# DeltaNet inverse on one core: the next D of a level by a product and a VectorE sum instead of a transpose

## The reference, cut to what matters

```python
def _gdn_chunked(q, k, v, beta, g, s0):
    ...
    decay = jnp.exp(jnp.where(incl, gc[..., :, None] - gc[..., None, :], -jnp.inf))
    kb = k * beta[..., None]
    lmat = jnp.where(strict, jnp.einsum("bhnik,bhnjk->bhnij", kb, k) * decay, 0.0)
    tinv = lax.linalg.triangular_solve(eye + lmat, jnp.broadcast_to(eye, lmat.shape), left_side=True,
                                       lower=True, unit_diagonal=True)
    u = tinv @ (v * beta[..., None])
    w = tinv @ (kb * jnp.exp(gc)[..., None])
    ...
```

## Time and profile before

| | |
|---|---|
| median of 3 runs | 2289.26 us (2286.62 to 2290.01) |
| profiled execution, its own time | 2281.79 us |
| its span, first to last instruction | 2279.9 us |
| PE busy | 2070.7 us (91%) |
| DVE busy | 984.4 us (43%) |
| ACT busy | 535.7 us (23%) |
| POOL busy | 267.5 us (12%) |
| mean granted clock of PE | 0.953 of full speed |
| inverses and chains of the 8 heads | 733 to 1412 us of the span |

### The profile page before, as it was taken

One profiled execution on the slowest core, in us unless ns is written; L12 is line 12 of the kernel. 1 busy time (PEld: TensorE's weight loads), 2 busy tenths in 40 slices (PEclk: granted clock), 3 DMA queues, 4 the chain that ended last, 5 costly groups with the idle time before them and its releaser, 6 DMA issues. The chain is left out here.

```text
span 2279.9 us, 28981 instructions
## 1 busy us (share of the span) xinstructions
PE 2070.7 (91%) x11714; PEld 1230.2 (54%) x11714; DVE 984.4 (43%) x1928; ACT 535.7 (23%) x1299; POOL 267.5 (12%) x333
## 2 busy tenths in 40 slices
PE   3799999999978999999999988999999794999985
PEld 1555555555544666667667665556555443443432
DVE  4355546556554465565654653000000186222224
ACT  1231423314212434344334343000000000111111
POOL 0020020110201111111021021000000000321102
PEclk9899999999989999999999999999999895999998
DMA  8120021201102101101011011982440734699973
GB/s 307 53 65 23 24 65 47 56 10 47 47 0 79 29 15 42 29 15 31 19 37 29 16 42 47 321 230 83 132 117 1 263 148 194 236 398 404 401 316 143
DMA packets 177812, 260.05 MB, mean 114 GB/s; under 512 B 14759, under 2 KB 146664, under 8 KB 163344
## 3 DMA queue, kind: packets, MB, share of 16 engines
q1 hardware_dynamic: 151096, 218.91, 28.0%
q10 hardware_dynamic: 18488, 23.54, 3.6%
q0 software_dynamic: 8096, 15.75, 1.9%
HBM read 231.65 MB, written 39.10 MB: 119 GB/s over the span
## 5 line engine op out<-in xcount | busy, mean ns | idle before, releaser
L678 PE MATMUL bank<-hT,shared 128*128 128x512 f32 x384 | 188.1, 619 | 7.8 <-DMA shared<-in_w_in_dram 7.8
L1504 PE MATMUL bank<-hT,shared 128*128 128x512 f32 x384 | 169.3, 594 | 2.6 <-DVE xT L1877 1.8
L2476 PE MATMUL bank<-ring,xgT 128*64 128x512 f32 (+1 forms) x416 | 150.2, 627 | 13.2 <-DMA ring<-in_w_exp_up_dram 10.1
L1559 PE MATMUL bank<-wz,hT 128*128 128x512 f32 x320 | 153.7, 618 | 0.0
L2058 DVE SCALAR_TENSOR_TENSOR prod<-gth,bank 128x512 f32<-128x512 f32 x16 | 11.0, 688 | 272.1 <-PE bank L2028 272.1
L1504 PEld LDWEIGHTS bank<-hT,shared 128*128 128x128 f32 x384 | 71.1, 190 | 84.5 <-issue 84.3
L2028 PE MATMUL bank<-yT,wm 128*128 128x512 f32 x256 | 111.2, 592 | 0.0
L2476 PEld LDWEIGHTS bank<-ring,xgT 128*64 128x64 f32 (+1 forms) x416 | 57.0, 165 | 95.6 <-issue 95.6
L1270 DVE TENSOR_TENSOR X<-bank,negm 128x512 f32<-128x512 f32 (+1 forms) x120 | 67.8, 598 | 91.3 <-PE bank L754 91.0
L678 PEld LDWEIGHTS bank<-hT,shared 128*128 128x128 f32 x384 | 67.3, 192 | 67.4 <-issue 54.7
L2028 PE MATMUL bank<-hT,wm 128*128 128x512 f32 x224 | 98.0, 595 | 0.0
(11 more groups left out here) (417 smaller groups left out, 3560.0 us busy)
## 6 DMA issues: line engine op xcount, KB each, us to landing
shared<-in_w_in_dram SPq DMA_DIRECT2D x62, 512.0 KB, 5.6
ring<-in_w_exp_gate_dram SPq DMA_DIRECT2D x26, 1024.0 KB, 12.5
ring<-in_w_exp_up_dram SPq DMA_DIRECT2D x26, 1024.0 KB, 18.9
ring<-in_w_exp_down_dram SPq DMA_DIRECT2D x26, 1024.0 KB, 14.7
aw<-in_w_ada_dram SPq DMA_DIRECT2D x8, 2048.0 KB, 11.2
yd<-mzero ACTq DMA_DIRECT2D x1, 16128.0 KB, 107.1
aw<-in_w_ada_dram SPq DMA_DIRECT2D x8, 1024.0 KB, 18.0
wz<-in_w_in_dram SPq DMA_DIRECT2D x4, 2048.0 KB, 8.0
```

Source lines behind the costliest of these rows:

```text
L678: last = pe.matmul(bank[LATB[j]][:, :], wof(j)[:, k, :], hT[:, k, SEQ:T], start=(k == 0), stop=(k == KD - 1), skip_group_check=True)
L1504: pe.matmul(bank[a][:, :], wn(n)[:, k, :], hT[:, k, SEQ:T], start=(k == 0), stop=(k == KD - 1))
L1559: last = pe.matmul(bank[Z][:, :], hT[:, k, t * P:(t + 1) * P], wz[:, k, :], start=(k == 0), stop=(k == KD - 1), skip_group_check=True)
L2476: last = pe.matmul(bank[2 + slot][at, :], xgT[:, slot, k, at], wgu[w][:, k, :, :], start=(k == 0), stop=(k == KD - 1))
```

## The change

Of a level below the last one, D is no longer made by transposing the new DT. A new `blocks_D` on PE multiplies DT and X of the level (the old DT, the masked X) into `xdv(g)`, right behind `blocks_DT` of the same group. For g = 0 and 1 this is the amount by which D grows: VectorE adds it to D_ in a new `add_D`. For g = 2, whose X holds the identity, it is the new D itself, and ScalarE copies it as before. `turn_D` stays for the first D of a head. `keep_DT` waits for `blocks_D` too, since it overwrites the DT that `blocks_D` reads; `blocks_DT` of the next level waits for `keep_DT`; `blocks_X` of the next level waits for `add_D` or the copy. On VectorE `add_D` of g = 0 stands between the masks of g = 1 and g = 2, that of g = 1 behind the mask of g = 2, ahead of the level's other work. The places of the filling stay, with those of `turn_D` gone. The added counter `g_Dadd` is declared in a hunk left out here.

```diff
--- before.py
+++ after.py
...
@@ -746,7 +746,12 @@
                 def blocks_X(h, l, g):
 
                     u0, m = GROUPS[g]
-                    pe.wait_ge(s["g_Dkept"], 18 * h + 3 * l + g + 1)
+                    if l == 0:
+                        pe.wait_ge(s["g_Dkept"], 8 * h + g + 1)
+                    elif g < 2:
+                        pe.wait_ge(s["g_Dadd"], 10 * h + 2 * l + g - 1)
+                    else:
+                        pe.wait_ge(s["g_Dkept"], 8 * h + l + 3)
                     for u in range(m):
                         a, b = same(u0 + u), other(u0 + u)
                         if l < LEVELS - 1:
@@ -760,6 +765,8 @@
 
                     u0, m = GROUPS[g]
                     pe.wait_ge(s["g_Xkept"], 18 * h + 3 * l + g + 1)
+                    if l > 0:
+                        pe.wait_ge(s["g_DTkept"], 18 * h + 3 * l + g - 2)
                     for u in range(m):
                         a, b = same(u0 + u), other(u0 + u)
                         if l < LEVELS - 1:
@@ -769,11 +776,17 @@
                             last = pe.matmul(tiles4(dtv(g))[a, u, b], X[b, u0 + u, a], DT[b, u0 + u, b], start=True, stop=True, skip_group_check=True)
                     last.then_inc(s["g_DT"], 1)
 
-                def turn_D(h, g, l):
+                def blocks_D(h, l, g):
 
                     u0, m = GROUPS[g]
-                    if l is not None:
-                        pe.wait_ge(s["g_DTkept"], 18 * h + 3 * l + g + 1)
+                    for u in range(m):
+                        for c in (same(u0 + u), other(u0 + u)):
+                            last = pe.matmul(tiles4(xdv(g))[c, u, c], DT[c, u0 + u, c], X[c, u0 + u, c], start=True, stop=True, skip_group_check=True)
+                    last.then_inc(s["g_Dturn"], 1)
+
+                def turn_D(h, g):
+
+                    u0, m = GROUPS[g]
                     for u in range(m):
                         last = pe.transpose(xdv(g)[:, u * P:(u + 1) * P], DT[:, u0 + u, :], C(C_ID))
                     last.then_inc(s["g_Dturn"], 1)
@@ -838,24 +851,19 @@
                     for g, (u0, m) in enumerate(GROUPS):
                         pe.wait_ge(s["g_D2"], 3 * h + g + 1)
                         pe.matmul(dtv(g), C(C_ID), flat(DT[:, u0:u0 + m, :]), start=True, stop=False, skip_group_check=True)
-                        turn_D(h, g, None)
+                        turn_D(h, g)
                     for g in range(3):
                         blocks_X(h, 0, g)
                     for l in range(LEVELS):
                         inner = l < LEVELS - 1
-                        blocks_DT(h, l, 0)
-                        fill(l, 0)
-                        blocks_DT(h, l, 1)
-                        fill(l, 1)
+                        for g in range(3):
+                            blocks_DT(h, l, g)
+                            if inner:
+                                blocks_D(h, l, g)
+                            fill(l, g)
                         if inner:
-                            turn_D(h, 0, l)
-                        blocks_DT(h, l, 2)
-                        fill(l, 2)
-                        if inner:
-                            turn_D(h, 1, l)
                             blocks_X(h, l + 1, 0)
                             fill(l, 3)
-                            turn_D(h, 2, l)
                             blocks_X(h, l + 1, 1)
                             blocks_X(h, l + 1, 2)
                             fill(l, 4)
@@ -1009,18 +1017,13 @@
                 def keep_D(h, turn, g):
                     u0, m = GROUPS[g]
                     act.wait_ge(s["g_Dturn"], 18 * h + turn + 1)
-                    if turn < 3 * (LEVELS - 1):
-                        act.copy(D_[:, u0:u0 + m, :], tiles4(xdv(g))).then_inc(s["g_Dkept"], 1)
-                    else:
-                        for u1, k in kinds(g):
-                            a = same(u1)
-                            last = act.copy(D_[a, u1:u1 + k, a], tiles4(xdv(g))[a, u1 - u0:u1 - u0 + k, a])
-                        last.then_inc(s["g_Dkept"], 1)
+                    act.copy(D_[:, u0:u0 + m, :], tiles4(xdv(g))).then_inc(s["g_Dkept"], 1)
 
                 def keep_DT(h, l, g):
                     u0, m = GROUPS[g]
                     act.wait_ge(s["g_DT"], 18 * h + 3 * l + g + 1)
                     if l < LEVELS - 1:
+                        act.wait_ge(s["g_Dturn"], 18 * h + 3 * l + g + 4)
                         act.copy(DT[:, u0:u0 + m, :], tiles4(dtv(g))).then_inc(s["g_DTkept"], 1)
                     else:
                         for u1, k in kinds(g):
@@ -1056,15 +1059,12 @@
                             raw_ctx_v(n)
                         if more and l == 4:
                             tanh(n, Q)
-                        if l < LEVELS - 1:
-                            keep_D(h, 3 * l + 3, 0)
-                        elif more:
+                        if more and l == LEVELS - 1:
                             keep_knT(n, 1 - par)
                         keep_DT(h, l, 2)
                         if more and l == 5:
                             square(n, 1 - par, Q)
                         if l < LEVELS - 1:
-                            keep_D(h, 3 * l + 4, 1)
                             if more and l == 2:
                                 if not first:
                                     act.wait_ge(s["g_head"], h)
@@ -1257,8 +1257,15 @@
                         st.wait(2 - g)
                         TT(out=DT[:, u0:u0 + m, :], in0=D_[:, u0:u0 + m, :], in1=cst[:, C_ID:C_ID + 1, :].broadcast_to([P, m, P]), op=ALU.add).then_inc(s["g_D2"], 1)
 
+                def add_D(h, l, g):
+                    u0, m = GROUPS[g]
+                    dve.wait_ge(s["g_Dturn"], 18 * h + 3 * l + g + 4)
+                    TT(out=D_[:, u0:u0 + m, :], in0=D_[:, u0:u0 + m, :], in1=tiles4(xdv(g)), op=ALU.add).then_inc(s["g_Dadd"], 1)
+
                 def mask_X(h, l):
                     for g, (u0, m) in enumerate(GROUPS):
+                        if g == 2 and l < LEVELS - 1:
+                            add_D(h, l, 0)
                         dve.wait_ge(s["g_X"], 18 * h + 3 * l + g + 1)
                         if l == LEVELS - 1:
                             for u1, k in kinds(g):
@@ -1298,6 +1305,8 @@
                     convolve(h, V)
                     for l in range(LEVELS):
                         mask_X(h, l)
+                        if l < LEVELS - 1:
+                            add_D(h, l, 1)
                         if l == 0:
                             silu(h, par, V)
                             if not first:
```

More of the change, by code:

```diff
@@ L622, in deltanet @@
                  "g_silu", "g_sq", "g_sumk", "g_sumq", "g_kturn", "g_vturn", "g_ssk", "g_ssq", "g_rn", "g_kn", "g_v", "g_knturn", "g_knT", "g_cur", "g_gm",
-                 "g_bm", "g_seg", "g_dec", "g_KQ", "g_att", "g_attm", "g_D2", "g_Dturn", "g_Dkept", "g_X", "g_Xkept", "g_DT", "g_DTkept",
+                 "g_bm", "g_seg", "g_dec", "g_KQ", "g_att", "g_attm", "g_D2", "g_Dturn", "g_Dkept", "g_Dadd", "g_X", "g_Xkept", "g_DT", "g_DTkept",
                  "g_KS", "g_QS", "g_R", "g_qs", "g_vnew", "g_vn", "g_vd", "g_O", "g_SU", "g_state", "g_osum", "g_qsadd", "g_oss", "g_osc",
```

## The result

The changed kernel takes 2274.84 us (median of 6 runs, 2271.7 to 2279.26) against 2289.33 (6 runs, 2286.62 to 2290.68) for the kernel before: ratio 0.9938, 95% interval 0.9925 to 0.995. It is faster by 14.5 us, where 4.3 slower was forecast with a range down to 2281. In a second set, 6 runs of the changed kernel beside 21 of the kernel before, the ratio is 0.9963 (0.9945 to 0.9982) and the medians, 2275.24 and 2282.54, differ by 7.3 us; the kernel before alone had moved, from 2289 to 2283.

The account below looks back on a forecast made before the run. The prediction took PE's queue to bound heads 0 to 6 and latencies head 7. It summed -1.3 (queue), +3.6 (waits) and +2.0 (head 7) to +4.3 us on 2289.3: 2293.6, with 2281 to 2304 for 8 in 10.

Parts of the forecast that it names:

- What bounds the kernel: DeltaNet heads: PE busy 85.3 of 87 us, VectorE 50.5; only head 7, without filling, is set by latencies.
- the shortened way from X to D: Heads 0 to 6: a copy and a hop fewer, covered by filling; PE waited only 0.8 + 1.6 us there.
- PE's own queue: PE, 5 levels of 8 heads: 57 us out, 54 in; by levels -0.18 a head, -1.3 us for seven.
- rival 3: PE: block instructions behind blocks cost 0.029 us, 46 us for the 1600 instead of 54, giving 2285.6; chance 0.05.
- The waits: PE waiting behind VectorE's order: 0.3 ahead of level 5, 0.25 ahead of the turned output, 3.6 us in all.
- Head 7: Head without filling: -1.0 from levels 0 and 1, +2.6 in level 2, +0.4 in levels 3 and 4; +2.0 us.
- The predicted cost of `mask_att`: Head 7, level 2: VectorE's masks 2.1, sums 1.3, `mask_att` 3.3, idle 0.7 make 7.4 against 4.75, +2.6 us.
- The clock: Heads 2 to 6: a short half-clock stretch of PE costs 1.7 us a head; five were taken again.
- Rival 2: PE's short half-clock stretches go, wholly or mostly, as in heads 0 and 1: 2285.1 us; chance 0.15.

Follow-up runs that it names:

- e9: Changed kernel with work not needing the sum moved into VectorE's idle 1.5 us, and the tanh of Q ahead of a ScalarE copy: 2268.23 us, 0.9922 against kernel before.
- e2: The changed kernel, unchanged, run for a second trace: 2275.24 us, 0.9963 against the kernel before.
- e4: Changed kernel with one unread 512-column identity product added in PE's 1.12 us wait, heads 0 to 6: 2269.15 us, 0.9933 against the kernel before.
- e10: Changed kernel with VectorE's work reordered, the unread identity product added, and head 7's `mask_att` moved from level 2 to level 0: 2268.84 us, 0.9918 against kernel before.
- e3: Kernel before with one unread 512-column identity product added in PE's 1.12 us wait, heads 0 to 6: 2277.32 us, 0.9969 against the kernel before.
- e5: Kernel before with every block product of the MT times D step issued twice: heads of 92.36 us against 87.09.

## Why the prediction was wrong, step by step

**What bounds the kernel: right.** PE's queue sets heads 0 to 6; the shortened way from X to D paid nothing there as such.

**PE's own queue: the term that failed, by its size.** The wrong step is the price of a block instruction that stands behind blocks, "0.033 each ... I take 0.034"; the runs show 0.029. The step took the slope from the groups of 8 and 24, and the group of 24 held a wait for ScalarE's copy. The slope from 8 to 16, which I had put down as a rival's low bound at (0.61 - 0.38) / 8 = 0.029, was the right one, and the groups of 32 and 40 of the changed kernel, 1.07 and 1.31, lie near it. For level 1 the miss is 0.08 + 0.07 + 0.14 = 0.29 of 10.78, which leaves 10.49; 10.52 came. Levels 2 and 3 are shorter by the same, 0.29 and 0.28, where they were to stay within 0.1. Over a head PE's queue changed by -0.95 less the waits of 0.40 + 0.12, which is -1.47 against the -0.18 predicted: 1.3 us a head, 9 us for seven, enough to turn the sign of the sum. That 1600 block instructions at 0.029 are 46 us and 400 transposes with their changes of form 57 is rival 3, to which I gave 0.05; I had weighed the longer lever of the step from 8 to 24 and not asked what its last 8 instructions wait for.
Of the 57 us out, 400 x 0.109 = 44 are transposes and 13 are changes of form. The added 46 us are more than the 44, so that without the changes of form the queue would gain nothing. The Trainium skill, in "TensorEngine Tiling (Array Packing)", section "Key Properties", has it that a change of tiling mode drains TensorE; the 0.61 against 0.51 for the same 16 instructions agrees. The 60 cycles for a product that the same page of the Trainium skill has in "Instruction Overhead", 25 ns at full clock by my estimate, are below every slope here, 0.0264 to 0.0294, even taken for one of the two instructions of a float32 product.

**The waits: right in place and near in size.** 0.3 and 0.25 were put ahead of level 5 and of the turned output; 0.40 and 0.12 came, 3.5 us in all against 3.6. Levels 1 to 3 had none. e9 shows that both come from the order of VectorE's work.

**Head 7: right for level 2, the total partly by luck.** +2.0 predicted; the two traces of the changed kernel have 39.91 and 37.29, those before 35.70 and 37.39, a difference of 2.05 in the mean. But the two of one kernel differ by as much, with the granted clock (0.83 and 0.91 after, 0.95 and 0.91 before), and the two at 0.91, 37.29 after and 37.39 before, are equal. The predicted cost of `mask_att` is there. Level 2 takes 7.12 (1360.20 to 1367.32), the same in the traces e2 and e4; 7.4 was predicted, and it was 4.75:

```profile
1367.32 1.12 PE L774 MATMUL bank<-DT,X 64*64 64x64 f32 x16 [2.45 <-DVE X L1277]
```

Levels 3 and 4 were to take 4.85. Level 4 takes 4.39, less than the 4.60 before. Level 3 takes 5.50, since a half-clock stretch starts behind the 2.45 us wait in each of these traces; in e10, without that wait, it takes 4.67. The prediction had no such stretch in its head 7.

**The clock: left open in the prediction, and it moved.** Five heads had the stretch before and I took five again; two traces of the changed kernel have three, -3.4 us. Rival 2 was right in kind, with two of the five stretches gone rather than all; e3 and e4 show their place. Why it is two isn't settled.

The sum with what was measured: -6.65 for seven heads, -3.4 for the clock, +2.05 for head 7 makes -8.0, the last two terms as means of two traces each. From the first inverse to the start of the merge the traces have 682.74 and 685.73 us before, 677.05 and 675.30 after, -8.1 in the mean, and the second comparison of medians has -7.3.

**What stays open** is the rest of the first comparison's 14.5 us. It lies in the kernel before, whose median was 2289.3 in that set and 2282.5, 2283.9 and 2286.4 in the three later sets, which ran on three chips (5, 7 and 1); the chip of the first set is not on record, so a difference of chips is not ruled out. Single runs reach from 2276 to 2291. They follow the mean granted clock: 0.956 in the run of 2276.16 us and 0.950 in that of 2291.35. No run near 2290 was traced, so in which stage its half clock lies isn't shown.

## What to carry to other kernels

Where an engine's queue is the bound, price an added or removed instruction by start-to-start differences between groups of which nothing waits: take each group's last operand, find who writes it and when, and use only those that are ready. Put work of one form together: here 13 of the 57 us taken out were changes of form, more than the 11 us by which the queue got shorter. When a step is put ahead of other work on an engine in order, look at what it waits for, and fill that idle time with what doesn't depend on it; here that was worth 0.68 us a head beyond the change itself.

## What the runs showed of the hardware that I had not expected

A wait of 1.12 us of PE, once a head, cost not only itself: in heads 2 to 6 of the kernel before the granted clock fell to half just behind it, so that the eight instructions behind it took 3.47 us in place of 1.99 and the head 1.7 us more. Filling 0.86 us of the wait with a product whose result nobody reads removed it (88.77 to 87.10 us). The same wait is followed by the stretch in five heads of the kernel before, three of the changed one, none of e5's and none of e9's, so that a small change elsewhere in a head can bring or take 1.7 us a head. Of two kernels that differ by one such detail, the medians can differ by more than the detail's own cost: 6.1 us between the changed kernel and the same with the product.
